# Two queues for the expert weights: five of twelve units move from SyncE to ScalarE

## The reference, cut to what matters

```python
def expert_block(args):
    xb, e = args
    hh = jax.nn.silu(xb @ w_gate[e]) * (xb @ w_up[e])   # 1024 -> 2 x 256
    return hh @ w_down[e]                               # 256 -> 1024
ys = lax.map(expert_block, (xs, blk_expert)).reshape(p_slots, d)
y = jnp.zeros((n + 1, d), ys.dtype).at[slot_tok].add(ys * slot_w[:, None])[:n]
```

## Time and profile before

| | |
|---|---|
| time, median of 3 runs | 1847.31 us (1847.21 to 1848.0) |
| the profiled execution's own time | 1850.71 us |
| its span (first to last instruction) | 1848.9 us |
| PE busy, share of the span | 91% |
| ACT busy, share of the span | 35% |
| read from HBM | 524.10 MB, mean 284 GB/s |

### The profile page before, as it was taken

The page is one execution under the profiler, slowest core; times in us unless marked ns, Lnnn a source line. Parts: engine busy times, 40 slices in busy tenths (PEclk is TensorE's granted clock), DMA queues, the critical chain, the costliest instruction groups (busy, mean ns, idle before and its releaser), DMA issues.

```text
span 1848.9 us, 31186 instructions
## 1 busy us (share of the span) xinstructions
PE 1680.2 (91%) x12410; PEld 1209.6 (65%) x12410; DVE 831.7 (45%) x1501; ACT 653.1 (35%) x1175; POOL 63.4 (3%) x58
## 2 busy tenths in 40 slices
PE   8999788887979999988887878999999999999997
PEld 8995434342435869534343433499998989999897
DVE  5652122121214754322121212279776646886663
ACT  4422111111103643211110111166557645655763
POOL 1100000000001000000000000010001110000110
PEclk9999888898989999999898889999999999999999
DMA  8669999999999324999999999935542243554232
GB/s 316 236 266 414 421 422 421 421 421 421 421 422 411 116 68 154 414 421 421 422 421 421 421 421 422 374 103 170 180 165 91 94 159 120 176 170 151 92 115 92
DMA packets 89224, 526.42 MB, mean 285 GB/s; under 512 B 10032, under 2 KB 10288, under 8 KB 39728
## 3 DMA queue, kind: packets, MB, share of 16 engines
q1 hardware_dynamic: 89136, 525.19, 72.2%
HBM read 524.10 MB, written 1.05 MB: 284 GB/s over the span
## 4 chain that ended last, share of the span: by engine, by line
PE 56%; DMA 28%; DVE 6%; SPq 6%; ACT 2%; issue 1%; DVEq 0%
DMA ring<-experts 16%; PE banks L504 13%; DMA arena<-experts 11%; PE banks L508 11%; PE banks L510 10%; PE banks L509 10%; SPq L443 6%; PE banks L702 5%; PE banks L684 3%; PE banks L720 3%; DVE arena L1606 1%; DVE hT L1731 1%; DMA ring<-dense 1%; PE banks L565 1%; ACT arena L1445 1%
## 5 line engine op out<-in xcount | busy, mean ns | idle before, releaser
L508 PE MATMUL banks<-arena_parts,ring_parts 128*128 128x256 f32 (+1 forms) x1444 | 418.3, 290 | 9.3 <-ACT arena L1157 5.1
L510 PE MATMUL banks<-arena_parts,ring_parts 128*128 128x256 f32 (+1 forms) x1444 | 409.9, 284 | 0.0
L509 PE MATMUL banks<-arena_parts,ring_parts 128*128 128x256 f32 (+1 forms) x1444 | 409.3, 283 | 0.0
L504 PEld LDWEIGHTS banks<-arena 128*128 128x128 f32 (+1 forms) x2512 | 302.4, 191 | 56.3 <-issue 43.9
L504 PE MATMUL banks<-arena 128*128 128x128 f32 (+3 forms) x2512 | 335.7, 288 | 1.9 <-ACT arena L1157 1.4
L702 PE MATMUL banks<-ring,arena 128*32 128x512 f32 x1536 | 237.2, 720 | 104.9 <-DMA ring<-experts 104.7
L1157 ACT ACTIVATE arena<-banks 128x256 f32<-128x256 f32 (+6 forms) x370 | 158.7, 455 | 396.4 <-PE banks L504 162.1
L1586 DVE TENSOR_TENSOR ring_parts<-ring,ring_parts 128x1024 fp32r<-128x1024 f32 x204 | 245.8, 1238 | 98.8 <-ACT ring_parts L1157 86.8
L508 PEld LDWEIGHTS banks<-arena_parts,ring_parts 128*128 128x128 f32 x1444 | 273.3, 189 | 17.8 <-issue 8.7
L1157 ACT ACTIVATE ring_parts<-ring 128x1024 fp32r<-128x1024 f32 x208 | 215.3, 1055 | 182.3 <-DMA ring<-dense 181.0
L509 PEld LDWEIGHTS banks<-arena_parts,ring_parts 128*128 128x128 f32 x1444 | 273.6, 189 | 0.3
(11 more groups left out here) (223 smaller groups left out, 1573.3 us busy)
## 6 DMA issues: line engine op xcount, KB each, us to landing
ring<-experts SPq DMA_DIRECT2D x192, 1024.0 KB, 26.5
arena<-experts SPq DMA_DIRECT2D x160, 1024.0 KB, 22.4
ring<-dense SPq DMA_DIRECT2D x224, 512.0 KB, 4.9
at<-experts SPq DMA_DIRECT2D x16, 1024.0 KB, 24.2
x<-experts SPq DMA_DIRECT2D x16, 1024.0 KB, 22.2
consts<-consts_in SPq DMA_DIRECT2D x1, 1414.0 KB, 13.0
vecs<-vecs_in SPq DMA_DIRECT2D x1, 1125.5 KB, 15.4
hT<-h_in SPq DMA_DIRECT2D x2, 544.0 KB, 4.4
```

Source lines behind the costliest of these rows:

```text
L504: return pe.matmul(o, lhsT, rhs, start=(k == 0), stop=(k == n - 1))
L508: pe.matmul(o, lhsT[0], rhs[0], start=(k == 0), stop=False)
L509: pe.matmul(o, lhsT[0], rhs[1], start=False, stop=False)
L510: return pe.matmul(o, lhsT[1], rhs[0], start=False, stop=(k == n - 1))
```

## The change

SyncE's `quad_but_one` goes. ScalarE's loop is rewritten in pairs of quads, and behind each of the first 14 quads it starts units 7 to 11 of the quad after the next on its own queue, with the same two waits per unit. The last two quads start nothing. SyncE keeps units 0 to 6, and all of the first loads.

```diff
--- before.py
+++ after.py
@@ -442,25 +442,14 @@
                         is_used(pair, odd, u)
                         sp.dma_start(expert_slot(u), experts[layer, (pair * 2 + (odd + 1 + QUADS)) % QUADS, u]).then_inc(m[f"landed{u}"], 16)
 
-                def quad_but_one(pair, odd):
-
-                    for u in range(TWICE, QU):
-                        is_used(pair, odd, u)
-                        sp.wait_ge(m[f"landed{u}"], (pair * 2 + (odd + 2)) * 16)
-                        sp.dma_start(expert_slot(u, odd == 1), experts[layer, (pair * 2 + (odd + 2)) % QUADS, u])\
-                          .then_inc(m[f"landed{u}"], 16)
-
                 sp.wait_ge(route["iter_ready"], layer + 1)
                 last = sp.value_load(n_last[0:1, layer:layer + 1], min_val=QUADS // 2 - 2, max_val=QUADS * ROUNDS // 2 - 2)
                 with sp.Fori(0, last) as i:
                     for odd in range(2):
                         next_quad(i, odd)
-                        quad_but_one(i, odd)
                 next_quad(last, 0)
-                quad_but_one(last, 0)
                 next_quad(last, 1)
                 next_quad(last + 1, 0)
-                quad_but_one(last, 1)
                 for u in range(QU):
                     use = (m["used"], last * (2 * QU) + (3 * QU + u + 1))
                     if u < RING:
@@ -1226,8 +1215,10 @@
 
                 tokens(1)
                 act.wait_ge(route["iter_ready"], layer + 1)
-                n = act.value_load(n_iter[0:1, layer:layer + 1], min_val=QUADS, max_val=QUADS * ROUNDS)
-                with act.Fori(0, n) as i:
+                last = act.value_load(n_last[0:1, layer:layer + 1], min_val=QUADS // 2 - 2, max_val=QUADS * ROUNDS // 2 - 2)
+
+                def quad(i):
+
                     act.wait_ge(s["used"], i * QU + 8)
                     act.activation(mo_silu[:, :], psum[:, 3, 0:256], ACT.Silu).then_inc(s["silu_done"], 1)
                     tokens(i + 2)
@@ -1236,9 +1227,25 @@
                     act.wait_ge(s["used"], i * QU + 10)
                     copy(mo_y[:, 0:512], psum[:, 4, :]).then_inc(s["ya_ready"], 1)
 
+                def load_quad_but_one(i, odd):
+
+                    for u in range(TWICE, QU):
+                        act.wait_ge(s["used"], i * QU + (u + 1))
+                        act.wait_ge(s[f"landed{u}"], i * 16 + 32)
+                        act.dma_start(expert_slot(u, odd == 1), experts[layer, (i + 2) % QUADS, u]).then_inc(s[f"landed{u}"], 16)
+
+                with act.Fori(0, last) as pair:
+                    for odd in range(2):
+                        quad(pair * 2 + odd)
+                        load_quad_but_one(pair * 2 + odd, odd)
+                for odd in range(2):
+                    quad(last * 2 + odd)
+                    load_quad_but_one(last * 2 + odd, odd)
+                for odd in range(2):
+                    quad(last * 2 + (2 + odd))
                 upper(after + 1)
                 for c in range(DC):
-                    act.wait_ge(s["add_done"], n * DC + (c + 2))
+                    act.wait_ge(s["add_done"], last * (2 * DC) + (4 * DC + c + 2))
                     if layer:
                         square(squares[:, c, 0:SEQ], hT[:, c, META:T])
                     else:
```

## The result

| | before | after |
|---|---|---|
| time, median | 1847.26 us (1846.4 to 1848.0, 4 runs) | 1866.38 us (1864.83 to 1867.58, 4 runs) |
| the profiled execution's own time | 1850.71 us | 1864.83 us |
| its span | 1848.9 us | 1862.9 us |

The ratio is 1.0103, with a 95% interval of 1.0086 to 1.0121: the change costs 19.1 us. The forecast was 1865, in a range of 1854 to 1880.

A forecast was written before the change was run, and what follows sets the result against it. The expert stages were taken to be bound by saturated DMA engines, plus PE's work behind the last byte. 7.9 + 8.5 + 2 x 0.5 = 17.4 us on the median 1847.3 gave 1864.7, say 1865 us; range 1854 to 1880.

The forecast's parts named there:

- Bytes and rate: In both expert stages: same transfers on saturated engines, so a second queue adds 0; bounds -14 to +29 us.
- The rival of a higher rate: In both stages two queues overlap the end and start of transfers: 1840 to 1858 us; chance 0.10, 0.06 for a gain.
- that of a lower one: In both stages the rate falls as engines change between two places in memory: 1870 to 1894 us; chance 0.13.
- SyncE's stalls: SyncE's issues, 1.93 us in the median with eleven units outstanding, probably get short; worth 0.
- ScalarE's issues: Five per quad for 14 quads, 2.2 us a quad, hidden in the gap in front of Silu; 0.
- The rival in which ScalarE is held up: Issues at 4.88 us each put Silu 9 us late in each quad: some 1880 us; chance 0.05.
- The hole behind quad 0: ScalarE can start (2, 7) only after its last copy, later than SyncE did: 0.5 us per stage, bounds 0 to 2.
- The order in the middle: Queues share evenly, quads alternate between about 27 and 33 us, two take 59.8 us as before; worth 0.
- the rival in which SyncE's queue goes first: Engines take SyncE's units ahead of ScalarE's, so (15, 7..11) stay last: 1847 to 1851 us; chance 0.10.
- The order at the end: At each stage's end (15, 0..6) land last, ahead of nearly a quad of work: 7.9 and 8.5 us.
- T + K: Stage end if quad 15 waits: T, all has landed; K, unit 6's landing to quad's end, 17.2 us.
- T - (7 + L) x 2.49 + K + 21.5: Stage end through quad 14; L, ScalarE's units left when (14, 6) lands, 1.8; put at T + 16.8.

The follow-up runs named there:

- e1: The changed kernel, but units 7 to 11 of quad 15, the last five of each stage, go back to SyncE's queue: 1850.59 us.
- e3: The kernel of e1, with units 7 to 11 of quad 2 started by SyncE too, right behind (1, 6): 1847.45 us.
- e2: The kernel before, all on SyncE's one queue, with (15, 7..11) started ahead of (15, 0..6): 1865.26 us.
- e5: The kernel before, one queue, with the single unit (15, 6) started behind (15, 7..11): 1866.43 us.
- e4: The kernel before, one queue, with (14, 7..11) started behind (14, 0..6), so the last 24 units go in order of use: 1843.9 us.

## Why the prediction was right, and where it was off

**What bounds the kernel.** Right. The windows over the middle of the first stage, the kernel before and then the kernel after:

```profile
190.00:560.00 370.00, 309.55 (x2051) 142.20 (x2052) 74.91 (x160) 48.95 (x75) 0.00 (x0) 0.87 1.01 421
```

```profile
190.00:560.00 370.00, 286.47 (x2008) 140.93 (x2012) 73.24 (x156) 37.16 (x64) 0.00 (x0) 0.86 1.01 422
```

A DMA share of 1.01 in both: the engines were as busy in the middle, and moved the same bytes in the same time.

**Bytes and rate, 0.** Right. 422 against 421 GB/s is 0.2%, at most 1 us of a stage. It comes back: in the windows 200 to 540 and 800 to 1140 us all six traces with one queue show 421, and the three with two queues (after, e1, e3) show 422. Before and after it is 143.27 against 143.38 MB in 340 us of the first stage, 0.1% or some 0.3 us of a stage. The trace of before had one queue, and its share of 1.01 alone couldn't show what a second one does; these traces do. The rival of a higher rate, which wanted 429 for a gain, and that of a lower one fall.

**SyncE's stalls, 0.** They went, as forecast: L443 from 900 to 1000 us shows 0.33 us for each issue after, against 1.93 in the median. In e3 they are gone too (0.33 us in the median of the same stretch), and it takes the time of before. The row is of the kernel after:

```profile
L443 SPq DMA_DIRECT2D ring<-experts x20: 332/333/333, 899.9 to 995.2; - x20
```

**ScalarE's issues, 0.** Right in the price: e3 keeps 120 of the 140 and costs nothing that its interval would show. The rival in which ScalarE is held up falls: an issue takes 0.34 us in the median of all 140 and 1.57 at most, not 4.88. Two details were wrong. Five issues take longer than the 2.2 us that were put in: 4.2 us behind quad 0 (158.8 to 163.0). And I had written that the new wait for a landing is over when ScalarE comes to it. It isn't always. Timeline of ACT in the kernel after, behind quad 1:

```profile
180.10 1.54 ACTq L1235 DMA_DIRECT2D arena<-experts  x3
181.93 0.34 ACTq L1235 DMA_DIRECT2D x<-experts  x1
185.85 0.34 ACTq L1235 DMA_DIRECT2D arena<-experts  x1
```

The fifth issue comes 3.6 us after the fourth is through (185.85 - 181.93 - 0.34), and behind quad 3 it is 4.6 us. ScalarE's next work is the Silu of quad 2, at 204.95, so it stays hidden.

**The hole behind quad 0.** The mechanism was right, the size too small: 0.5 us per stage was put in, and the windows show 1.2 to 1.3 us, inside the bound of 0 to 2. Windows of 1 us in the kernel after:

```profile
159.00:160.00 1.00, 1.00 (x12) 0.26 (x8) 0.00 (x0) 0.13 (x1) 0.00 (x0) 1.00 0.82 188
160.00:161.00 1.00, 1.00 (x16) 0.39 (x12) 0.69 (x1) 0.00 (x0) 0.00 (x0) 1.00 0.49 172
```

These two lack 0.48 of the 0.52 MB; from 161 on the rate is 377 or more. (1, 6) is started at 145.1 and lands 16.3 us later, at 161.4, but the rate falls off about two us before that, and what ScalarE starts at 158.8 brings the rate back only from 161 on. The step that was mis-sized is the 1.7 us for what lies before and behind the data, taken from a transfer of 256 KB: for these units it is 161.4 - 158.8 + 1.2 = 3.8 us, an estimate from the times above.

**The order in the middle, 0.** Right in the price. While both queues have work, they share evenly. The DMA view of the kernel after for 246 to 251 us (packets, MB, share):

```profile
q1 hardware_dynamic: 144, 1.05, 50.6%
q10 hardware_dynamic: 145, 1.06, 50.6%
```

That is the rule of the Trainium skill, page "DMA: Bandwidth & Descriptors", section "Queues, rings and completion order" (an engine takes its queues in turn); the trace agrees with it here, with 50.6% for each queue, and the rival in which SyncE's queue goes first is gone. Two landings on one queue are then 5 us apart. Timeline of PE in the kernel after, quads 2 and 3:

```profile
181.30 2.76 PE L691 MATMUL banks<-ring,arena 128*32 128x512 f32 x24
186.31 1.06 PE L691 MATMUL banks<-ring,arena 128*32 128x512 f32 x8 [2.25 <-DMA ring<-experts]
191.39 1.94 PE L691 MATMUL banks<-ring,arena 128*32 128x512 f32 x8 [4.01 <-DMA ring<-experts]
196.26 1.93 PE L691 MATMUL banks<-ring,arena 128*32 128x512 f32 x8 [2.94 <-DMA ring<-experts]
201.25 3.64 PE L691 MATMUL banks<-arena 128*32 128x512 f32 x16 [3.05 <-DMA arena<-experts]
219.13 5.33 PE L691 MATMUL banks<-ring,arena 128*32 128x512 f32 x48
```

Quad 2 takes 37.8 us and quad 3, up to 241.03, takes 21.9. I had forecast 33 and 27: (2, 6) was still (201.2 - 181.3) / 5 = 4.0 units away when quad 1 ended, and not 3.2. A part of this is the hole: 8.8 units were to be moved by the end of quad 1, but from the end of the hole (about 160.6) to 181.3 there is time for 8.3. The sum of quads 2 and 3 is 59.7 us, where 59.8 was worked out, so this costs nothing, however uneven it looks. The quads alternate to the end of the stage, by turns 34 to 38 us and 22 to 26 us, further apart than forecast, and unit 6 is 3.2 to 4.0 units away at the start of every even quad from 2 to 14.

**The order at the end.** This is the main term, and it held: T + 17.0 and T + 16.8, where T + 17.2 was taken; 7.7 and 8.1 us more than before, where 7.9 and 8.5 were. e1 shows that it is this order that costs the time in the changed kernel, and e2 and e5 show the mechanism by itself: what matters is when the last of units 0 to 6 of the last quad lands, and not how many are late.

The way in which the number came out was in part luck. The prediction took the later of two ends, T + K, in which quad 15 waits for unit 6, and named a wait of quad 15 for units 4 to 6 as a sign. That sign failed: quad 15 runs without a wait, since (15, 6) lands at 581.1 and its turn comes at 581.8. The two ends lay less than a microsecond apart. The end was set by the other path of the same sum, through quad 14: T - (7 + L) x 2.49 + K + 21.5, which had been put at T + 16.8. Two of its terms were off and cancelled. From the use of (14, 6) to the last landing are 581.1 - 557.9 = 23.2 us, not 21.9. K was 18.7 us in quad 14 (557.94 to 576.63), not 17.2 and above all of 16.2 to 18.0; the granted clock stood at 0.50, the lower of the two levels, from 552 to 560 us, while PE waited for units 5 and 6 (3.8 and 3.0 us), and the gather behind them took 6.4 us, where it took 5.6 in quad 15 at a clock of 1.00. Also, (14, 6) was (557.9 - 542.2) / 5 = 3.2 units away behind quad 13, the number that I had (in the second stage too); but the quads before had 3.7 to 4.0 more often, and with those the same sum gives T + 18.0 to T + 18.8, 1 to 2 us more per stage.

**The sum.** 17.4 us were forecast. The stages account for 17.8 us in the profiled executions: 7.7 and 8.1 us from the last landing to the end, and 1.7 and 0.3 us by which the last landing comes later, counted from the stage's first issue. The medians differ by 19.1. The order alone (e2) costs 18.2 by the medians and 16.7 by the lengths of its stages (456.5 and 457.5 us). What is left in e1 is 3.6 by the medians and nothing by the lengths. The sum by the medians, 21.8, is above 19.1, but each of the three intervals is some 3 to 6 us wide. So the end of the stages makes up 16 to 18 us, and the hole 0 to 4 us; the runs settle it no further.

## What to carry to other kernels

In this kernel, whose transfers are saturated in the stage, moving issues to a second queue changed little but the order in which data lands. In a like case, look for the price where that order meets the end of the stage. There, ask for each input when it lands at the latest and how much work hangs behind it: a single 1 MB unit with 18 us of work behind it, put last in each of the two stages, cost 19 us in all, and putting last what is used last, and cutting the work behind it, won 11. Check every input by this sum, not only the one that was late before; that is where the expectation of e4 failed.

## What the runs showed of the hardware

Two queues with work shared the 16 engines to 50.6% and 50.6%, at 421 to 422 GB/s together, where one queue moved 421. With two queues an issue took 0.34 us in the median on ScalarE's and 0.33 us on SyncE's; on the single queue, between 900 and 1000 us, it took 1.93 us in the median. There a unit landed 26.8 us behind its issue in the median, so some eleven were outstanding (26.8 / 2.49, an estimate). At the end of the stage, with a landing after 24.4 us, some ten, the issue on the same queue took 0.33 us. No run shows more closely where the change lies.
